# A hybrid RG-LRU and mLSTM step in fp32 on one core: VectorE's drains and low parts reordered at the seams of heads, in the fifth unit and in the last

## The reference, cut to what matters

```
u = rmsnorm(x)
xr, gr, xm, zm, pi, pf, ga, gb = split(u @ w_in)
y_a = rglru(conv4(xr)) * gelu(gr)
xc  = silu(conv4(xm))                     # 8 heads of 256
q, k, v = xc @ wq, xc @ wk, xm @ wv       # per head
y_b = sigmoid(zm) * mlstm_chunkwise(q, k, v, pi, pf)
mix = sigmoid(ga) * (y_a @ wpa) + sigmoid(gb) * (y_b @ wpb)
x   = x + mix @ w_out
x   = x + relu(rmsnorm(x) @ w_up)**2 @ w_down
return rmsnorm(x), new states
```

## Time and profile before

| what | value |
|---|---|
| median of 3 runs | 2140.29 us (2139.29 to 2142.95) |
| the profiled execution | 2142.61 us |
| its span, first to last instruction | 2140.8 us |
| mean granted TensorE clock | 0.996 |
| TensorE busy | 2113.5 us (99%) |
| VectorE busy | 1467.0 us (69%) |
| GpSimd busy | 1246.8 us (58%) |
| ScalarE busy | 765.9 us (36%) |
| DMA | 269.95 MB, mean 126 GB/s |

### The profile page before, as it was taken

The page is one execution under the profiler, slowest core; times in us unless marked ns, Lnnn a source line. Parts: engine busy times, 40 slices in busy tenths (PEclk is TensorE's granted clock), DMA queues, the critical chain, the costliest instruction groups (busy, mean ns, idle before and its releaser), DMA issues.

```text
span 2140.8 us, 37683 instructions
## 1 busy us (share of the span) xinstructions
PE 2113.5 (99%) x14464; PEld 2088.1 (98%) x14464; DVE 1467.0 (69%) x1537; ACT 765.9 (36%) x1031; POOL 1246.8 (58%) x817
## 2 busy tenths in 40 slices
PE   9999999999999999999999999899999999999998
PEld 8999999999999999999999999899999999999988
DVE  6676776136887787797755298876867645558876
ACT  5443434213323423423423242334343434424332
POOL 3555564343653653553456686358777768788730
PEclk9999999999999999999999999999999999999999
DMA  3212113431322322222345344474545456626522
GB/s 137 68 55 70 59 55 98 149 100 46 115 73 66 114 73 76 99 94 89 115 167 192 108 165 151 140 245 155 190 150 191 150 184 227 231 77 238 179 67 84
DMA packets 120359, 269.95 MB, mean 126 GB/s; under 512 B 11808, under 2 KB 34464, under 8 KB 113984
## 3 DMA queue, kind: packets, MB, share of 16 engines
q1 hardware_dynamic: 75072, 125.81, 18.8%
q10 hardware_dynamic: 45184, 142.71, 18.1%
HBM read 188.09 MB, written 80.39 MB: 125 GB/s over the span
## 4 chain that ended last, share of the span: by engine, by line
PE 75%; DVE 16%; issue 3%; ACT 2%; DMA 2%; ACTq 1%; POOL 1%; DVEq 0%; SPq 0%; POOLq 0%
PE ps L1175 31%; PE ps L1494 24%; PE ps L1433 6%; PE ps L1591 4%; DVE vt L2444 4%; DVE acc L2447 3%; PE ps L1355 2%; DVE acc L2845 2%; PE ps L1389 1%; PE ps L1370 1%; DVE vt L2447 1%; PE ps L1392 1%; DMA last_x<-hid 1%; ACT vt L1640 1%; DVE bform_lo L2447 1%
## 5 line engine op out<-in xcount | busy, mean ns | idle before, releaser
L948 POOL TENSOR_TENSOR w_hi<-w_raw,ones 128x512 fp32r<-128x512 f32 x180 | 225.1, 1251 | 604.3 <-PE ps L1175 563.1
L1175 PE MATMUL ps<-u_hi,w_hi 128*128 128x364 f32 x1533 | 340.3, 330 | 1.5 <-issue 1.1
L1175 PE MATMUL ps<-u_hi,w_lo 128*128 128x364 f32 x1533 | 338.3, 329 | 0.0
L1175 PE MATMUL ps<-u_lo,w_hi 128*128 128x364 f32 x1533 | 337.9, 328 | 0.0
L951 POOL TENSOR_TENSOR w_lo<-w_raw,w_hi 128x512 fp32r<-128x512 f32 x180 | 325.3, 1807 | 14.1
L1175 PEld LDWEIGHTS ps<-u_hi,w_hi 128*128 128x128 f32 x1533 | 265.9, 188 | 2.7 <-issue 1.7
L1175 PEld LDWEIGHTS ps<-u_lo,w_hi 128*128 128x128 f32 x1533 | 266.6, 188 | 0.0
L1175 PEld LDWEIGHTS ps<-u_hi,w_lo 128*128 128x128 f32 x1533 | 266.5, 188 | 0.0
L1494 PE MATMUL ps<-form_hi,hi 128*128 128x272 f32 x784 | 162.1, 288 | 0.4 <-POOL lo L1063 0.4
L1494 PE MATMUL ps<-form_hi,w_hi 128*128 128x272 f32 x776 | 161.2, 289 | 1.1 <-DVE small L2447 1.0
L1494 PE MATMUL ps<-form_hi,lo 128*128 128x272 f32 x784 | 162.3, 288 | 0.0
(11 more groups left out here) (371 smaller groups left out, 4792.2 us busy)
## 6 DMA issues: line engine op xcount, KB each, us to landing
w_raw<-in_w SPq DMA_DIRECT2D x248, 256.0 KB, 2.6
form_lo<-hid_forms ACTq DMA_DIRECT2D x21, 1088.0 KB, 7.7
rstd<-in_w SPq DMA_DIRECT2D x50, 256.0 KB, 2.8
hid_forms<-acc ACTq DMA_DIRECT2D x12, 816.0 KB, 6.0
bc<-out_rows ACTq DMA_DIRECT2D x8, 1092.0 KB, 7.5
y_forms<-t_sums ACTq DMA_DIRECT2D x8, 1092.0 KB, 5.0
bform_lo<-y_forms SPq DMA_DIRECT2D x7, 1092.0 KB, 5.3
bform_lo<-y_forms ACTq DMA_DIRECT2D x7, 1092.0 KB, 6.0
```

The lines of the kernel that those rows point to most:

```text
L948: nc.gpsimd.tensor_tensor(w_hi[:, c, :], w_raw[:, c, :], one, ALU.mult).then_inc(s_whi, 1)
L1175: mm = nc.tensor.matmul(slots[slot][:, t, :], w, r(k)[:, t * TW:(t + 1) * TW], start=(k == 0 and n == 0), stop=(k == last_k and n == 2))
```

## The change

In VectorE's program: `z_out` can do one block alone, and at each seam its first block goes into `xm`, behind the silu product and ahead of the wait for `xc_hi`. In unit 4 the P2 quarter goes ahead of the low part of B22. In unit 7, `mix_row(4)` goes ahead of the unit's first quarter and `mix_row(5)` takes the place that `mix_row(4)` had; of the low parts only rows 1 and 2 stay ahead of the last two additions to `acc`; behind them come the low parts of rows 3 to 5, then `mix_row(6)` and `mix_row(7)`, and then the low parts of rows 6 and 7. In ScalarE's program, `mix_hi(5)` goes ahead of the high parts of the third and fourth output chunks, and the two residual loads wait for the last product of `y_b @ wpb` where they waited for the last `act_lo`, and go ahead of `mix_hi(6)`. In SyncE's program, the loads of the third and fourth output chunks go ahead of the four loads into `b_end_rows`.

```
--- before.py
+++ after.py
@@ -787,11 +787,11 @@
+        fetch(W_OUT + 2, 0, D_OUT + 1)
+        fetch(W_OUT + 3, 1, D_OUT + KB + 1)
         sp.wait_ge(s_mm, b_index(B_UNITS - 1, P2) + 1)
         for k in range(12, 16):
             b_row_load(k)
-        fetch(W_OUT + 2, 0, D_OUT + 1)
-        fetch(W_OUT + 3, 1, D_OUT + KB + 1)
@@ -2050,16 +2050,15 @@
         mix_hi(4)
+        mix_hi(5)
         out_hi(2)
         out_hi(3)
-        for n in range(5, KB):
-            mix_hi(n)
-        act.wait_ge(s_nlo, KB + KB)
+        act.wait_ge(s_mm, B_PRODUCTS)
         for half in range(2):
             load(x_t, ROWS[half], tmp[:, half, :], g_in[half])
+        mix_hi(6)
+        mix_hi(7)
@@ -2852,8 +2851,8 @@
-                xm(h + 1, c0 + 2, (a0 + 3, b0 + 3))
-                z_out(h + 1, c0 + 6)
+                xm(h + 1, c0 + 2, (a0 + 3, b0 + 3), lambda step: z_out(h + 1, c0 + 6, (0,)) if step == 5 else None)
+                z_out(h + 1, c0 + 6, (1,))
@@ -2920,13 +2919,15 @@
             if t >= 5 and step == 1:
-                mix_row(2 * (t - 5))
                 if t < B_UNITS - 1:
-                    mix_row(2 * (t - 5) + 1)
+                    mix_row(2 * (t - 5))
+                mix_row(2 * (t - 5) + 1)
...
+            if t == B_UNITS - 1:
+                mix_row(4)
...
-            b_step(t, 1)
+            if t != 4:
+                b_step(t, 1)
...
                 b_quarter(t, P2, s1, s1, 2)
+                if t == 4:
+                    b_step(t, 1)
@@ -2964,17 +2968,18 @@
                     b_quarter(t, P4, s2, s2, 5)
-                    for n in range(1, 5):
-                        mix_lo(n)
-                    mix_row(5)
-                    mix_lo(5)
+                    mix_lo(1)
+                    mix_lo(2)
                 b_added(t, b_snap4, n0, B_SECOND, 6, 3)
...
                 b_added(t, s2, n1, B_FIRST, 7, 4)
-        for n in (6, 7):
-            mix_row(n)
+        for n in (3, 4, 5):
             mix_lo(n)
+        mix_row(6)
+        mix_row(7)
+        mix_lo(6)
+        mix_lo(7)
```

4 lines of the change are left out of this document (2 added, 2 removed).

## The result

The changed kernel takes **2129.29 us** (median of 5 runs, 2125.61 to 2133.05); the kernel before, run beside it on the same chip, 2142.52 us (5 runs, 2139.29 to 2142.95). The ratio is 0.9945, 95% interval [0.9929, 0.9961]: faster by some 12 us. The forecast was 2128.3 us with 2125.5 to 2134.5 as its range.

A forecast was written before the change was run, and what follows sets the result against it. TensorE was taken as the bound, busy 2113.5 of 2140.8 us. The terms 3.5 + 0 - 0.6 + 4.6 + 2.8 + 1.7 summed to 12.0 us gained, giving a median of 2128.3 us, range 2125.5 to 2134.5.

The forecast's parts named there:

- The seams: Between heads, slot A's drain fills VectorE's pause before `xc_lo`, ending TensorE's waits for `acc`: 3.5 us gained.
- Unit 4: P2 quarter ahead of B22's low part: 0 us, ends 0.6 gained and 0.6 lost.
- The start of the projection: Last unit: two more row instructions ahead of the third quarter start the output projection 0.6 us later.
- The stall at row 6: In the output projection, TensorE's wait for row 6's `act_lo` goes: 4.6 us gained, no stall.
- The clock: Behind row 6, TensorE's clock stays at 2.4 GHz without the stall: 2.8 us gained.
- The residual addition: Before TensorE's second part of the output projection, earlier residual loads let slot A drain sooner: 1.7 us gained.
- The sum: All terms over the whole kernel: 12.0 us gained, 2140.8 becoming 2128.8 us, the median 2128.3 us.
- The port is lost whole: `mix_row(4)` in unit 7 gets nothing until GpSimd's splits end; projection 4.3 us later, gain 7.6 us; chance 0.15.
- Row 6 late still: Output projection still stalls 2.5 us at row 6, clock drop costing 2.8 more; gain 6.7 us; chance 0.10.
- The seams give nothing: At the seams another wait, by ScalarE's or GpSimd's work, ends 0.4 us later; gain 8.5 us; chance 0.05.
- slower: Last unit: row 11's load lands so late that P4's quarter holds TensorE; some 2145 us; chance 0.02.

The follow-up runs named there:

- `row11_first`: Changed kernel with the row loads of the last units ahead of the second output chunk on SyncE's queue; 2128.07 us, ratio 0.9937.
- `queue_back`: Changed kernel with the third and fourth chunk loads back behind the loads into `b_end_rows` on SyncE's queue; 2130.15 us (one run).
- `split_row5`: Changed kernel with the second instruction of `mix_row(5)` behind row 2's low part and `mix_hi(5)` behind the two output chunks' high parts; 2131.64 us, ratio 0.9958.
- `held_split_row5`: `split_row5` with GpSimd's splits of output chunks 5 and 6 also held until row 6's low part is done; 2127.18 us, ratio 0.9936.
- `seams_only`: Kernel before with only the drain moved at the seams of heads; 2136.93 us, ratio 0.9979.
- `unit4_only`: Kernel before with only unit 4's P2 quarter moved ahead of B22's low part; 2139.67 us, ratio 0.9994.
- `loads_late`: Changed kernel with the two residual loads and their wait back behind the last low part; 2130.59 us, ratio 0.9956.

## Why the prediction was right, point by point

**The seams** (3.5 forecast, 4.10 measured, outside the ends 2.4 to 3.8). The mechanism is as put. The term that was too small is the refill. A seam was costed at its idle time and 0.16 us; set matmul against matmul, the first one behind a wait starts that much late, and the second another 0.10 us. 2.4 + 7 x 0.26 is 4.2; measured are 4.10, and 0.09 more in the next column of the table, where the last seam's second matmul falls. The distance between the same instruction in two successive heads fell from 77.50 to 76.88 us in the middle heads, 0.62. The size was to be read in the earlier trace rows: two matmuls take 0.49 us ahead of the wait and 0.60 behind it.

**Unit 4** (0 forecast with 0.6 to either side). Right: nothing, 0.9994 [0.9985, 1.0002] alone.

**The start of the projection** (0.6 later forecast). The chain worked out holds nearly step by step. Brought to before's clock (4.53 us later), the third quarter ends at 1323.7, forecast 1323.6, and the projection starts at 1329.03, forecast 1329.0. Two steps inside it were different and cancel, since the instruction ends behind GpSimd's turn either way (`row11_first`): `mix_row(5)` had to wait 0.82 us for row 11, and its second instruction took 1.49 us, not 2.2. What the forecast had wrong is the base. It compared with a trace in which one row instruction took 4.94 us; without that oddity the start is 1.15 us later, not 0.6.

**The stall at row 6** (4.6 gained forecast, no stall). 0.34 us is left. The low part was ready at 1347.3 in before's clock, forecast 1346.6: `mix_row(6)` took 2.7 us and the low part of row 6 2.1 us, nearly as put, but the stretch began 0.2 us later and `mix_row(7)` took 4.3 us for 3.8. With 0.5 us to spare, that is what it cost. That it was not more is in part luck: the forecast gave the two low parts at 1330.4 the price of undisturbed ones without asking where GpSimd's chunk splits fall, and `queue_back` shows that this holds only with the chunk loads moved. No kernel here puts the whole of `mix_row(5)` alone back into this stretch, so what that one move is worth by itself was not measured; half of it is what `split_row5` puts back.

**The clock** (2.8 forecast). The stretch is at 1.00, as forecast. Set matmul against matmul with `held_split_row5`, whose first part is the shortest in any trace (24.24 us), before has 9.14 us too many: 0.10 at its start, 4.64 of stall, 2.80 at the lower clock, 1.59 at the drain. The changed kernel has 0.45, of which 0.34 at row 6 and 0.11 at its start, so 8.69 are gained of a forecast 9.1. But the 2.80 are no price of the clock alone. Behind the same stall `seams_only` and `unit4_only` lose 2.40 and 2.20 us up to the drain (in the latter 0.44 by a wait for the low part of row 7), then 2.04 and 2.33 at the drain, and their first parts are 33.26 and 33.36 us long, before's 33.38. The drain waited for a load issued behind the last low part, so what TensorE gained by a better clock it waited away there. The sum of these two terms is what the traces bear out, 4.39 us of a forecast 4.5; with the loads left in their place and the stall as it was, the clock would have given next to nothing, as these two kernels show.

**The residual addition** (1.7 forecast, 1.59 measured). Right, and `loads_late` shows that this edit is needed for it (1.77).

**The sum** was 12.0 and is 12.2 in the traces; the seams' 0.6 too little and the first part's 0.4 too much nearly offset each other, which is luck. (The range has a slip: the best ends give 2126.1, and one us more 2125.1, not 2125.5.) The term that the sum left out is the queue order of the two chunk loads: I costed it at nothing because the wait of ScalarE that it removes held nobody. It is worth 2.7 us, through GpSimd's splits and not through ScalarE.

**The rivals.** *The port is lost whole*: did not happen; the pair in the pause took 2.27 and 2.21 us, and the 4.94 us came back in none of the thirteen traces after the first. The reading of that row holds as far as it goes: GpSimd's three instructions beside it took 1.32, 1.31 and 1.32 us, the price that they have alone. Elsewhere in these stretches a VectorE instruction of 1.3 us that meets GpSimd's is slowed by 0.9 us or so, and one of GpSimd's of 1.3 us by 1.0, in turn. The Trainium skill (SBUF — State Buffer, "Who interferes with whom") says that such a pair contends, and, of VectorE's two-port modes, that the one that issues first has the port for its whole instruction and the other "fully blocks". The rows agree with both for one instruction at a time; that the turns alternate, which decides the price, is what they add. It also says that a VectorE instruction with at most one input in SBUF, outside its two-port modes, does not contend, and the first chunk split, 1.27 us beside quarters of 0.71, agrees. *Row 6 late still*: did not happen as the change stands, but with the chunks in the old order (`queue_back`, 2.81 us) or one instruction more in the stretch (`split_row5`, 2.70) it does; there is no margin left at that place (0.34 us of delay remains), and 0.10 was not too much for it. *The seams give nothing* and *slower*: no sign of either; row 11 landed at 1316.99, and its lateness was free.

## What to carry to other kernels

Filling an engine's pause is worth what the engines share, not the length of the pause: where two engines slow each other, idle time on one can be speed on the other, and 3.4 us filled gave 1.5. Ask of each instruction moved which instruction of the other engine it now stands beside; the quarters, which read one operand from PSUM, stood beside GpSimd's split for nothing (0.71 and 1.27 us). Take a wait's price from the starts of the matmuls around it and not from its idle time, ask whether a later wait would swallow what an earlier one gives, and check the baseline trace for one-off instructions before measuring against it.

## What was not expected

- **An idle time that cost nothing.** Removing a 0.82 us wait for a load moved nothing (`row11_first`, 175.30 against 175.32 us), since the row instruction behind it ends with GpSimd's turn, whether it starts early and takes 2.2 us or late and takes 1.49.
- **Which stalls the clock follows.** It went to the lower level, 1.2 GHz, after idles of 4.47 us (0.50), of 2.70 us (0.51, `split_row5`), and after 2.19 us at 1356.98 in `seams_only` (0.58 in the row below) and 2.49 us at 1360.58 in `unit4_only` (0.51), where an earlier low stretch had ended only some us before. It stayed at 1.00 after 2.81 us in `queue_back`, and after 1.91 in `loads_late`. So the length of one idle does not settle it; what does, these runs do not show.

The granted clock in `seams_only` behind its second wait:

```profile
1357.60:1361.00 3.40, 3.40 (x14) 3.40 (x14) 2.40 (x4) 2.44 (x4) 0.00 (x0) 0.58 0.42 166
```

- **A single execution is off by up to 4.4 us in a place that no edit touches.** The profile of after was 17.1 us better and the change 12.2. Only distances cut at the program's own instructions showed which part was which.
- **Left open.** Why one row instruction of before took 4.94 us was not found. It started 0.03 us behind an instruction of GpSimd's (1317.42 and 1317.39), and so did the same one in `seams_only` (1313.27 and 1313.24), where it took 2.43 us. It did not come back in any trace.
